# mLSTM mixer without states between token tiles, and a turned copy of the inverse in the delta-net levels, in a two-block kernel

## The reference, cut to what matters

```python
def step(carry, inp):                      # one chunk of 128 tokens
    C, n, m = carry
    b = jnp.cumsum(lfx, axis=-1)
    dmat = where(lower, b[..., :, None] - b[..., None, :] + lix[..., None, :], -inf)
    inter = b + m[..., None]
    m_t = jnp.maximum(inter, jnp.max(dmat, axis=-1))
    w = jnp.exp(dmat - m_t[..., None]);  a = jnp.exp(inter - m_t)
    s = (qx @ kx.T) * w
    num = a[..., None] * (qx @ C) + s @ vx
    den = a * (qx @ n) + jnp.sum(s, axis=-1)
    h = num / jnp.maximum(jnp.abs(den), jnp.exp(-m_t))[..., None]
    g = b[..., -1:] - b + lix
    m_new = jnp.maximum(b[..., -1] + m, jnp.max(g, axis=-1))
    C_new = exp(b[..., -1] + m - m_new) * C + (kx * exp(g - m_new)).T @ vx
    ...
h_c, s_f, s_b = bidir_mlstm(context, zero, zero)    # only s_f, s_b are used
h_l, _, _     = bidir_mlstm(latents, s_f, s_b)
```

## Time and profile before

| | us |
|---|---|
| median of three runs (lowest, highest) | 1845.86 (1845.23, 1846.47) |
| the profiled execution, its own time | 1843.97 |
| its span in the trace | 1842.2 |
| mean granted TensorE clock in it | 0.966 |

### The profile page before, as it was taken

The page is one execution under the profiler, slowest core; times in us unless marked ns, Lnnn a source line. Parts: engine busy times, 40 slices in busy tenths (PEclk is TensorE's granted clock), DMA queues, the critical chain, the costliest instruction groups (busy, mean ns, idle before and its releaser), DMA issues. The chain is left out here.

```text
span 1842.2 us, 28309 instructions
## 1 busy us (share of the span) xinstructions
PE 1731.2 (94%) x12118; PEld 1583.0 (86%) x12118; DVE 1010.8 (55%) x1188; ACT 754.9 (41%) x949; POOL 238.8 (13%) x193
## 2 busy tenths in 40 slices
PE   7999998999897799999999999998898999979998
PEld 7997988998684589988998999887688988969996
DVE  4663447554744555557555555557456464665543
ACT  4462233443344333443444444344345344444442
POOL 0123404000400220003000300011000230020000
PEclk8999999999998999999999999999798899989999
DMA  7553157665467667656764766555045124446652
GB/s 219 160 183 126 59 183 207 183 184 194 173 205 274 203 197 218 183 184 181 218 182 164 204 185 178 189 160 183 1 138 160 47 81 137 157 119 182 183 183 91
DMA packets 329282, 306.59 MB, mean 166 GB/s; under 512 B 12065, under 2 KB 287046, under 8 KB 329030
## 3 DMA queue, kind: packets, MB, share of 16 engines
q1 hardware_dynamic: 324358, 296.20, 52.3%
q10 hardware_dynamic: 4528, 7.54, 1.2%
q0 software_dynamic: 272, 1.05, 0.1%
HBM read 303.70 MB, written 1.05 MB: 165 GB/s over the span
## 5 line engine op out<-in xcount | busy, mean ns | idle before, releaser
L388 DVE TENSOR_TENSOR wlo<-raw,whi 128x2048 fp32r<-128x2048 f32 x247 | 587.4, 2381 | 386.5 <-ACT whi L382 386.3
L411 PE MATMUL ps<-ah,whi 128*128 128x256 f32 x2384 | 684.5, 287 | 9.7 <-DVE wlo L388 8.9
L411 PE MATMUL ps<-al,whi 128*128 128x256 f32 x2384 | 678.9, 285 | 0.0
L411 PE MATMUL ps<-ah,wlo 128*128 128x256 f32 x2384 | 678.7, 285 | 0.0
L382 ACT CAST whi<-raw 128x2048 fp32r<-128x2048 f32 x247 | 470.3, 1906 | 226.7 <-PE ps L435 157.1
L411 PEld LDWEIGHTS ps<-ah,whi 128*128 128x128 f32 x2384 | 462.5, 194 | 14.7 <-issue 10.0
L411 PEld LDWEIGHTS ps<-al,whi 128*128 128x128 f32 x2384 | 462.3, 194 | 1.6 <-issue 1.4
L411 PEld LDWEIGHTS ps<-ah,wlo 128*128 128x128 f32 x2384 | 462.0, 194 | 0.0
L752 ACT ACTIVATE f_sig<-ps 128x256 f32<-128x256 f32 x110 | 42.3, 384 | 372.0 <-PE ps L411 354.5
L435 PE MATMUL ps<-whi,fh 128*128 128x512 f32 x440 | 171.5, 390 | 0.0
L435 PE MATMUL ps<-wlo,fh 128*128 128x512 f32 x440 | 171.2, 389 | 0.0
(11 more groups left out here) (356 smaller groups left out, 1906.9 us busy)
## 6 DMA issues: line engine op xcount, KB each, us to landing
raw<-in_f_w SPq DMA_DIRECT2D x132, 512.0 KB, 4.7
raw<-in_w_a SPq DMA_DIRECT2D x132, 512.0 KB, 4.5
raw<-in_w_ada SPq DMA_DIRECT2D x72, 512.0 KB, 4.7
raw<-in_w_in SPq DMA_DIRECT2D x68, 512.0 KB, 4.5
raw<-in_w_b SPq DMA_DIRECT2D x66, 512.0 KB, 4.5
raw<-in_a_w_in SPq DMA_DIRECT2D x32, 512.0 KB, 5.1
raw<-in_b_w_qkv SPq DMA_DIRECT2D x24, 512.0 KB, 4.7
raw<-in_a_w_out SPq DMA_DIRECT2D x8, 512.0 KB, 4.2
```

The lines of the kernel that those rows point to most:

```text
L388: dve.tensor_tensor(wlo[:, c % RING, :], raw[:, r % RING, :], whi[:, c % RING, :].bitcast(F32), ALU.subtract).then_inc(S("lo_ready"), 1)
L411: last = pe.matmul(out_ap, a, b, start=(i == 0), stop=(i == n - 1))
```

## The change

Levels. The product y and the DVE subtraction from `inv` go. When DVE has updated `invt`, PE transposes it (4 transposes for a group, `level_turn_pe`) and ACT copies the result to `inv` (`level_turn_act`), in levels 1 to 5 of both tiles.

Context. The maxima and cumulative sums run over all 256 tokens in each direction (`m_rows_pe` adds the other tile's whole sum by a matmul with ones), so that one factor for each token brings it to the final state. An update sums both tiles in PSUM, 8 updates of 8 records each; DVE only copies. The row work stands in c_v: `m_rows_pe(0)` behind cut 0, `m_cols_pe(0)` and two blocks of k_tok behind cut 2, two behind cut 3. Updates 0 and 1 stand behind turn 7, 2 to 4 behind l_k cuts 0, 1 and 3, 5 to 7 behind l_v cuts 0, 1 and 2. The latents' k_tok and their 8 updates go.

Latents. Both tiles start from the context state, and each reads the keys of the other tile where the direction calls for it: in tile t direction 1−t has a second product. Three weight pieces per tile (own forward, own backward, other tile): the mask is added to the exponent in PSUM by an fp32r matmul, ACT takes 12 exponentials of 128x128 with a bias, DVE multiplies. POOL has no part in it. The denominators are made once for four heads. m_rows(1) stands behind l_q cut 0; behind l_f cut 0 stand m_cols(1), cm and st of tile 0.

```diff
-            if s < 6:
-                pe.matmul(bank(y, HG)[:, h, :], invt[:, tt, HG * g + h, :], wlev[:, g, h, :],
+    def level_turn_pe(pe, tt, s, g):
+        if s < 6:
+            pe.wait_ge(*S("invtup", step(tt, s, g) + 1))
+            for h in range(HG):
+                last = pe.transpose(bank((2, 5)[g], HG)[:, h, :], invt[:, tt, HG * g + h, :], ident)
+    def level_turn_act(act, tt, s, g):
+            act.wait_ge(*S("inv_ps", 10 * tt + 2 * (s - 1) + g + 1))
+            act.copy(inv[:, tt, heads(g), :], bank((2, 5)[g], HG)).then_inc(S("invup"), 1)
...
     def update_pe(pe, u):
+        for tt in range(TT):
+            i = 2 * u + tt
+            pe.wait_ge(*S("kw", i + 1))
+            for kk in range(2):
+                last = pe.matmul(ps[4 + 2 * (u % 2) + kk][:, 0:W1], kw[i % 2][:, kk * P:kk * P + P],
+                                 v_aug[:, tt, h, :], start=(tt == 0), stop=(tt == 1))
...
+    def part_pe(pe, t, d):
+        other = d == 1 - t
+        for h in range(NH):
+            i = 4 * (2 * t + d) + h
             wait_from(pe, *S("nq", i))
             for kk in range(2):
                 last = pe.matmul(ps[0][:, 0:W1], qt[:, 2 * h + kk, tile], cell[:, d, h, kk, :], ...)
             wait_from(pe, *S("num", i))
+            last = pe.matmul(ps[1][:, 0:W1], s_t(t, d)[:, h, :], v_aug[:, t, h, :], start=True, stop=not other)
+            if other:
+                last = pe.matmul(ps[1][:, 0:W1], s_t(t, 2)[:, h, :], v_aug[:, 1 - t, h, :], ...)
...
 PE order
+        stream_pe(pe, "c_v", ah, al, context_rows)
         turn_pe(pe, 7, xn)
+        update_pe(pe, 0)
+        update_pe(pe, 1)
         gates_pe(pe, 2, 3)
+        stream_pe(pe, "l_k", ah, al, updates({0: 2, 1: 3, 3: 4}))
+        stream_pe(pe, "l_v", ah, al, updates({0: 5, 1: 6, 2: 7}))
+        stream_pe(pe, "l_q", ah, al, lambda j: m_rows_pe(pe, 1) if j == 0 else None)
         stream_pe(pe, "l_f", ah, al, only=[0])
+        m_cols_pe(pe, 1)
+        cm_pe(pe, 0)
+        st_pe(pe, 0)
         stream_pe(pe, "l_f", ah, al, only=[1])
+        part_pe(pe, 0, 0)
+        stream_pe(pe, "l_o", ah, al, only=[0])
+        cm_pe(pe, 1)
+        st_pe(pe, 1)
+        part_pe(pe, 0, 1)
+        stream_pe(pe, "l_o", ah, al, only=[1])
+        part_pe(pe, 1, 0)
+        stream_pe(pe, "l_o", ah, al, only=[2])
+        part_pe(pe, 1, 1)
+        stream_pe(pe, "l_o", ah, al, only=[3])
 ACT order in l_v
+        def value_cuts(j, c, b):
+            cut_ahead(act, c)
+            if j < 3:
+                update_act(act, 5 + j)
 ACT and DVE order of the parts
+        lat_in_act(act, "l_o", 1)
+        cut_ahead(act, segs["l_o"].cut[1])
+        part_act(act, 1, 0)
+        cut_ahead(dve, segs["l_o"].cut[1])
+        part_dve(dve, 1, 0)
```

More of the change, by code:

```diff
@@ L2139, in m_cols_pe @@
+    def m_cols_pe(pe, n):
+        if n == 0:
+            pe.wait_ge(*S("m_wk", 2))
+            out_, kinds = ps[4], [m_r0]
+        else:
+            pe.wait_ge(*S("m_a", 2))
             pe.wait_ge(*S("m_em", 1))
[L2140 removed]
+            pe.wait_ge(*evicted("l_q", 3))
+            out_, kinds = ps[1], [m_r1, m_a, m_s1]
         for d in range(2):
             for tt in range(TT):
[L2143 to L2146 removed]
@@ new lines, in update_pe @@
+        h = u // 2
+        if u == 0:
+            pe.wait_ge(*evicted("c_v", 3))
+            pe.wait_ge(*S("ones_col", 1))
+            pe.wait_ge(*S("m_cols", 1))
+            pe.wait_ge(*S("m_next", 2))
+            pe.wait_ge(*S("k_tok", 4))
+        wait_from(pe, *S("cell", 2 * (u - 1)))
+        for tt in range(TT):
+            i = 2 * u + tt
[3 more added lines that the diff above has]
+                                 v_aug[:, tt, h, :], start=(tt == 0), stop=(tt == 1))
+            last.then_inc(S("cell_ps"), 1)
@@ new lines, in piece, with mask_dve, cm_pe @@
+    def piece(t, i):
+        return ((0, t, 6), (1, t, 7), (1 - t, 1 - t, 2))[i]
+    def mask_dve(dve):
+        dve.wait_ge(*S("row_am", 4))
+        dve.wait_ge(*S("row_b", 4))
+        dve.tensor_scalar(identr[:, :], ident, -1.0, None, ALU.mult).then_inc(S("m_mask"), 1)
+    def cm_pe(pe, t):
+        tile = slice(t * P, t * P + P)
+        pe.wait_ge(*S("m_scan", 4))
+        pe.wait_ge(*S("m_mask", 1))
+        if t == 0:
+            pe.wait_ge(*S("cell", 16))
+            pe.wait_ge(*evicted("l_q", 3))
+        for i in range(3):
+            d, _, b = piece(t, i)
+            wait_from(pe, *S("w_exp", 12 * (t - 1) + 4 * i + 4))
+            if i < 2:
+                left, right = ((identr, negr), (negr, identr))[d]
+                pe.matmul(bank(b, NH), left[:, :], over(right[:, :]), start=True, stop=False)
+            for h in range(NH):
+                last = pe.matmul(bank(b, NH)[:, h, :], tab("sel", 4)[0:4, h, :], m_cm1[0:4, d, tile],
+                                 start=(i == 2 and h == 0), stop=(h == NH - 1))
+            last.then_inc(S("cm_ps"), 1)
@@ new lines, in st_pe @@
+    def st_pe(pe, t):
+        if t == 0:
+            pe.wait_ge(*S("conv3", 12))
+            pe.wait_ge(*S("m_rows", 3))
+            pe.wait_ge(*S("cell", 16))
+        else:
+            pe.wait_ge(*S("s_t", 3))
+        for b, k in ((4, t), (5, 1 - t)):
+            for h in range(NH):
+                for kk in range(2):
+                    last = pe.matmul(bank(b, NH)[:, h, :], kt[:, 2 * h + kk, k * P:k * P + P],
+                                     qt[:, 2 * h + kk, t * P:t * P + P], start=(kk == 0), stop=(kk == 1))
+        last.then_inc(S("st_ps"), 1)
```

523 lines of the change are left out of this document (231 added, 292 removed).

## The result

The changed kernel takes 1837.45 us, the median of 11 runs (1828.5 to 1844.29), against 1846.47 us for the kernel before, the median of 11 runs of its own (1838.83 to 1850.84). The ratio is 0.9945, with a 95% interval of 0.993 to 0.9959. Run once more beside the last experiments it gave 1834.82 us and 0.9946 (0.9925 to 0.9967). So it is faster by 0.55%, some 10 us, where 18 were forecast. Every ratio here is taken against the kernel before, run on the same chip in the same rounds.

The account below looks back on a forecast made before the run. PE, busy 94% of the span, was taken as the bound through its work, idle stretches and clock. The steps summed to −18.0 us from 1843.97, giving 1826.0 profiled; 1.9 more for the median gave 1828, range 1810 to 1843.

Parts of the forecast that it names:

- main case: Whole kernel: the summed steps hold, giving 1828 us, range 1820 to 1836; chance 0.50.
- rival C: Whole kernel: each short wait costs clock, +10 in l_v and +5 at the parts, 1843 us; chance 0.22 including E.
- c_v to the gates: Context: row work and half of k_tok move into c_v, turn 7 sets the end; 68.3 to 39.1 us, −29.2.
- gates and l_k: Gates start at a fallen clock, l_k gains three updates; 34.4 to 41.0 us, +6.6.
- l_v: Three updates add 5.2 us, their waits for scaled keys 7.5, a clock fall 1.0; +13.7.
- l_q: m_rows(1) there has 16 matmuls for 12; +0.9 us.
- l_f to l_br: Latents: updates and k_tok go, other-tile products and new waits come; 99.0 to 94.9 us, −4.1.
- l_br: The 1.5 us wait for `wlo` goes as the head norm's PE work comes earlier; −1.5 us.
- levels: Delta-net levels: y goes, transposes come; 0.52 us saved in each of 5 in tile 0, 0.36 in tile 1; −4.4.
- 1.0 put down for a fall: l_v: a one in five chance of 5 us lost to the clock at the 2.5 us key waits; 1.0 us.
- second half-clock stretch behind cm(1): Latents: a second half-clock stretch behind cm(1) and in the waits, by chance; 2.7 us.
- parts' waits for m_nq: Latents: parts start behind ACT's and DVE's cut work, so PE waits 3.9 + 3.1 + 3.9 + 0.1; sum 10.9 us.

Follow-up runs that it names:

- the first repair: Changed kernel with DVE making the low part of l_k cut 2 behind turn 7 instead of in front: 1834.01 us, 0.9937 of the kernel before.
- Undoing the waits alone: Changed kernel with ACT scaling the keys of updates 5 to 7 ahead of the l_v casts: 1822.2 us, 0.9879 of the kernel before.
- mixer-alone: Changed kernel with the levels of the kernel before put back: 1837.5 us, 0.9949 of the kernel before.
- the exchanges of keys and parts together: Changed kernel with keys and parts ahead of the casts, and DVE's l_k cut 2 rest behind turn 7: 1813.95 us, 0.9826 of the kernel before.

## Why the prediction was right, and where it was off

The direction was right and the time lies in the stated range of 1810 to 1843, but the gain came out at 9 to 10 us and not 18. 1837.45 is 1.45 above the range of the main case alone (1820 to 1836) and just below that of rival C (1838 to 1846): the wide range held it, not the sum. By the steps of the sum, profile against profile:

| step | forecast | measured |
|---|---|---|
| c_v to the gates | −29.2 | −29.3 |
| gates and l_k | +6.6 | +6.1 |
| l_v | +13.7 | +15.4 |
| l_q | +0.9 | +1.0 |
| l_f to l_br | −4.1 | −3.8 |
| l_br | −1.5 | −1.5 |
| mixer together | −13.6 | −12.1 |
| levels | −4.4 | −2.4 |

**Context.** Right, and for the reason given: turn 7's chain ended the stretch at 12.4 us, and `al` was late next. What the step missed is that after the change it wasn't one chain. The prediction took turn 7 from before as it was; ACT's new order, with four keys ahead of the turn's casts, made a second chain of the same length. It cost nothing in the sum, and made the first repair worthless. The prediction also speaks of three stretches at the half clock; the profile of before has five in the mixer. The other two lie around the 7.6 us wait in turn 7 (13.7 us) and the 6.8 us wait in l_f (10.2 us):

```profile
1284.00:1297.00 13.00, 6.55 (x30) 4.43 (x31) 6.03 (x9) 5.93 (x9) 4.46 (x4) 0.50 0.24 81
1417.20:1427.20 10.00, 5.61 (x27) 5.64 (x28) 2.29 (x1) 5.92 (x11) 0.00 (x0) 0.50 0.27 87
```

So all three long waits of before had the clock at half around them, where the prediction names one. They bear on rival C and not on the sum.

**Gates and l_k, l_v.** The clock was down when the gates began, as taken. The three waits in l_v measured 2.54, 2.55 and 2.54, against 2.5 forecast. The 1.0 put down for a fall was too small. Five profiles hold these waits unedited; each had at least one fall in l_v, of 3.4 us, and two had two. A fall costs 1.7 us of work, so 2.4 in the mean. Undoing the waits alone gave 9.9 us of l_v.

**Latents.** Near the forecast in this profile by two errors that cancel: part (0,0) took 8.9 where 9.05 was forecast, parts (1,0) and (1,1) 11.5 and 10.3 where 10.1 and 9.05 were, because the clock fell in them; the second half-clock stretch behind cm(1) did not come in this execution. In the mixer-alone profile it did, for 6.8 us; with that run's other falls its mixer was 5.9 us longer. The parts' waits for m_nq were taken at 10.9 us and measured 8.3, while a part of own keys without any wait takes 6.2 us and not 5.2.

**Levels.** The term was mis-sized. I had a level of 7.1 us go to 6.5, and that it did, from the earlier trace rows to this:

```profile
170.12 2.02 PE L1172 MATMUL ps<-inv,x 128*128 128x128 f32 x16
...
176.66 2.02 PE L1172 MATMUL ps<-inv,x 128*128 128x128 f32 x16
```

6.54 us. But the shown level was the one with most to gain. The next one went from 6.66 to 6.43, the one before from 6.65 to 6.43. Two steps failed. "ACT's copy is hidden by the other group's w" is one: PE waited for it in front of w in six places, 0.3 to 0.4 us each, 2.5 in all, two of them in tile 0 and four in tile 1. The other is the saving of one row, which I let stand for five: of the three levels of tile 0 without such a wait two gained 0.2 us, and the one whose row was read 0.6.

**From the profile to the runs.** The profile gave −13.2, the runs −9.0 by the medians and −10.2 by the ratio. The forecast for the profiled execution was 1826.0 and it took 1830.86: 1.5 us more in the mixer, 2.0 in the levels, and 1.3 behind the levels, where the 48 narrow matmuls in front of c_k alone had 6.8 us at half clock against 3.4 and lost 1.6. The other half of the miss is the step from the profiled execution to the median. It was put at 1.9, as before the change, and measured 6.6: the profiled execution had the highest mean clock of the eleven, 0.970, where their median was 0.966. That its profile came so near to the steps of the sum is in part luck.

Rival C was thus no rival but a part of the answer: it described what happens in some executions. The forecast gave it 0.22 as if it came always or never, and at +10 in l_v, where the falls cost 2.4. By the four profiles of this mixer and the two of the one before, the change takes 10 us of work and idle away, and gives back about 1.5 to the clock (41.4 us of busy time at half clock in the mean against 38.5). With 2.4 in the levels that is an estimate of 11 us, near the 9 to 10 of the runs.

## What to carry to other kernels

When work is moved under another engine's work, read the order of the engine that feeds it. Here both feeders, ACT and DVE, came to the fed step just behind a 1.9 us cast and a 2.3 us subtraction that nobody was in need of for two more cuts. Exchanging two lines on ACT was worth 12 us, give or take 5, about as much as the whole change, and the exchanges of keys and parts together some 22 (with a third edit that showed nothing by itself). Of two engines that feed one step, one edit shows nothing while the other is as late.

Price a new wait of PE at more than its length. In l_v three waits of 2.5 us brought 2.4 us of lost clock in the mean. In the whole mixer the four profiles with the waits had 41.4 us of busy time at half clock in the mean and the one without them 29.4, so about 6 us of time went with 15.4 us of waits. That is an estimate from one profile on one side.

## What the runs showed of the hardware

The clock isn't the same function of the code in each execution. The same mixer instructions ran at a mean granted clock of 0.93, 0.93, 0.92 and 0.91 in four profiles, or 286.4, 286.1, 291.0 and 292.3 us. Their waits in l_v and in the parts are equal to 0.02 us; the third has one DVE cut moved, and 4.6 us in front of the gates instead of 4.8.

An idle PE of 2.5 us had a fall of the clock within 2 us of its end in seven of the fifteen such waits in l_v, in five profiles. The first of the three had one in all five, the other two in two of ten; why is open.

The 48 matmuls of 16 columns stand at three places of the program. In each of the thirteen profiles and at each place the clock was at half in them or from at most 0.5 us behind them, for 3.4 to 17.1 us, with 0 to 4.8 us of idle PE in front. Where they were moved into l_k, the fall moved with them.

Transposes among other matmuls had no fall: tile 1's levels ran at 1.00 with 40 of them.
